# A two-layer transformer trunk on one core: the rotary embedding as three VectorE operations in place of twelve on GpSimd

## What is computed

```python
def apply_rope(t, cos, sin):
    half = ROT_DIM // 2                 # ROT_DIM = 32
    t1 = t[..., :half]
    t2 = t[..., half:ROT_DIM]
    return jnp.concatenate([t1 * cos - t2 * sin, t2 * cos + t1 * sin, t[..., ROT_DIM:]], axis=-1)

q = apply_rope(rms_norm(qkv[:, :, g, 0], q_gain[g]), cos, sin)      # layer 0, group g
k = apply_rope(rms_norm(qkv[:, :, g, 1], k_gain[g]), cos, sin)
k = rope_pairs(rms_norm((h @ w_k)..., k_gain), cos, sin)            # layer 1
q = rope_pairs(rms_norm((h @ w_q)..., q_gain), cos, sin)
```

## Time and profile before

| What | Value |
|---|---|
| median of three runs | 2704.87 us (2704.64, 2704.87, 2712.0) |
| span of the profiled execution | 2709.5 us |
| TensorE matmuls busy | 2437.8 us (90%), 10901 |
| TensorE weight loads busy | 1986.8 us (73%) |
| VectorE busy | 1856.3 us (69%), 2225 |
| ScalarE busy | 1152.7 us (43%), 1762 |
| GpSimd busy | 268.2 us (10%), 368 |
| mean DMA rate | 246 GB/s |
| w_lo, line 905 | 800 operations, 978.8 us |
| adaptive norm, line 924 | 194 operations, 457.2 us |

### The profile page before, as it was taken

One profiled execution on the slowest core, in us unless ns is written; L12 is line 12 of the kernel. 1 busy time (PEld: TensorE's weight loads), 2 busy tenths in 40 slices (PEclk: granted clock), 3 DMA queues, 4 the chain that ended last, 5 costly groups with the idle time before them and its releaser, 6 DMA issues.

```text
span 2709.5 us, 31158 instructions
## 1 busy us (share of the span) xinstructions
PE 2437.8 (90%) x10901; PEld 1986.8 (73%) x10901; DVE 1856.3 (69%) x2225; ACT 1152.7 (43%) x1762; POOL 268.2 (10%) x368
## 2 busy tenths in 40 slices
PE   0389989898899999999997768888899999999999
PEld 0378778776787888888886656766687888788887
DVE  7778676777778677777785657766887555455554
ACT  1345545454543443443444344444354344343442
POOL 1122121230100000000002341110000000000000
PEclk9699999999899999999998889999999999999999
DMA  9777575776788777787775556663977555555554
GB/s 362 283 262 287 221 294 210 304 268 215 282 301 312 268 287 265 276 309 246 280 290 199 205 191 249 257 246 132 351 278 265 187 190 182 172 186 186 188 186 155
DMA packets 150355, 665.66 MB, mean 246 GB/s; under 512 B 16752, under 2 KB 17104, under 8 KB 120784
## 3 DMA queue, kind: packets, MB, share of 16 engines
q1 hardware_dynamic: 150224, 663.95, 67.1%
HBM read 661.78 MB, written 2.10 MB: 245 GB/s over the span
## 4 chain that ended last, share of the span: by engine, by line
PE 63%; issue 16%; DVE 9%; POOL 8%; ACT 3%; DMA 2%; SPq 0%; DVEq 0%; POOLq 0%; ACTq 0%
PE main L384 20%; PE main L385 20%; PE main L386 20%; DVE acc L924 4%; POOL rot L1387 2%; POOL rot L1386 2%; DVE w_lo L905 2%; PE tr L397 2%; POOL rot L1388 1%; POOL rot L1389 1%; ACT w_hi L676 1%; DMA w_raw<-w 1%; POOL st_a L1393 1%; PE tr L439 1%; DMA ada_raw<-ada 1%
## 5 line engine op out<-in xcount | busy, mean ns | idle before, releaser
L905 DVE TENSOR_TENSOR w_lo<-w_raw,w_hi 128x1024 fp32r<-128x1024 f32 x800 | 978.8, 1228 | 625.7 <-ACT w_hi L676 624.6
L676 ACT ACTIVATE w_hi<-w_raw 128x1024 fp32r<-128x1024 f32 x800 | 847.0, 1061 | 1305.6 <-PE main L386 1171.5
L384 PE MATMUL main<-w_hi,hT_hi 128*128 128x512 f32 x2176 | 879.4, 404 | 9.0 <-DVE hT_lo L1081 4.0
L385 PE MATMUL main<-w_lo,hT_hi 128*128 128x512 f32 x2176 | 858.5, 395 | 3.9 <-issue 3.9
L386 PE MATMUL main<-w_hi,hT_lo 128*128 128x512 f32 x2176 | 857.3, 394 | 0.0
L384 PEld LDWEIGHTS main<-w_hi,hT_hi 128*128 128x128 f32 x2176 | 417.1, 192 | 98.4 <-DVE w_lo L905 6.0
L386 PEld LDWEIGHTS main<-w_hi,hT_lo 128*128 128x128 f32 x2176 | 415.2, 191 | 93.8 <-issue 4.1
L385 PEld LDWEIGHTS main<-w_lo,hT_hi 128*128 128x128 f32 x2176 | 416.6, 191 | 84.5 <-issue 1.2
L924 DVE SCALAR_TENSOR_TENSOR acc<-ada_raw,c_act,acc 128x2048 f32<-128x2048 f32 x194 | 457.2, 2357 | 7.1 <-DMA ada_raw<-ada 5.6
L384 PE MATMUL main<-w_hi,mid_hi 128*128 128x512 f32 x1024 | 405.8, 396 | 0.0
L386 PE MATMUL main<-w_hi,mid_lo 128*128 128x512 f32 x1024 | 403.6, 394 | 0.0
(11 more groups left out here) (161 smaller groups left out, 1340.7 us busy)
## 6 DMA issues: line engine op xcount, KB each, us to landing
w_raw<-w SPq DMA_DIRECT2D x800, 512.0 KB, 4.2
ada_raw<-ada SPq DMA_DIRECT2D x208, 1024.0 KB, 6.3
qT<-ada SPq DMA_DIRECT2D x16, 1024.0 KB, 6.9
gate<-bias_rows SPq DMA_DIRECT2D x4, 1024.0 KB, 7.2
xs<-x SPq DMA_DIRECT2D x1, 2048.0 KB, 9.9
out<-xs SPq DMA_DIRECT2D x4, 512.0 KB, 5.2
gains_sb<-gains SPq DMA_DIRECT2D x1, 640.0 KB, 4.5
st_a<-lamb SPq DMA_DIRECT2D x1, 256.0 KB, 5.5
```

Source lines behind the costliest of these rows:

```text
L384: pe.matmul(acc_ps[:, :], hi[:, kt, tc], w_hi[:, s, wc], start=(kt == 0), stop=False)
L385: pe.matmul(acc_ps[:, :], hi[:, kt, tc], w_lo[:, s, wc], start=False, stop=False)
L676: act.activation(w_hi[:, s, :], w_raw[:, s, :], ACT.Copy).then_inc(hi_done, 1)
L905: dve.tensor_tensor(w_lo[:, s, :], w_raw[:, s, :], w_hi[:, s, :].bitcast(F32), ALU.subtract).then_inc(lo_done, 1)
```

## The change

The tables become `cos8` and `sin8`, filled for all eight pairs of tile and head (128x256 each): the cosine twice in 32 columns, the sine once negated and once not. ScalarE fills them with six operations in place of two. The rotary embedding moves from GpSimd's queue into VectorE's `norm` step, right behind the normalization: a product of the first 32 elements of the eight heads with `cos8`, a product of the same elements with their halves swapped with `sin8`, and the sum of both in place. `read_out`, which frees the PSUM banks, is signalled by the first product, which waits for the norm's last operation; the sum waits for both products and signals `roped`. GpSimd keeps its other work (the staging of x and of the heads, line 1367). `rot` moves to another place in SBUF and is 128x512.

```diff
@@ tables
-        cos = sb("cos", [P, T * HALF])
-        sin = sb("sin", [P, T * HALF])
+        cos8 = sb("cos8", [P, T * MAPS, ROT])
+        sin8 = sb("sin8", [P, T * MAPS, 2, HALF])
-        rot = sb("rot", [P, T, 4, MAPS, HALF])
+        rot = sb("rot", [P, 2, T * MAPS, ROT])
@@ ScalarE, at the start
-            act.activation(sin[:, :], small[:, 0:T * HALF], ACT.Sin)
-            act.activation(cos[:, :], small[:, T * HALF:2 * T * HALF], ACT.Sin, bias=hpi_t[:, :],
-                           scale=-1.0).then_inc(trig_done, 1)
+            for t in range(T):
+                ang = small[:, t * HALF:(t + 1) * HALF].unsqueeze(1)
+                mag = small[:, (T + t) * HALF:(T + t + 1) * HALF].unsqueeze(1)
+                maps = slice(t * MAPS, (t + 1) * MAPS)
+                act.activation(sin8[:, maps, 0, :], ang.to_broadcast([P, MAPS, HALF]), ACT.Sin, scale=-1.0)
+                act.activation(sin8[:, maps, 1, :], ang.to_broadcast([P, MAPS, HALF]), ACT.Sin)
+                last = act.activation(cos8[:, maps, :].rearrange("p m (h e) -> p (m h) e", h=2),
+                                      mag.to_broadcast([P, 2 * MAPS, HALF]), ACT.Sin, bias=hpi_t[:, :], scale=-1.0)
+            last.then_inc(trig_done, 1)
@@ VectorE, norm
-                    last.then_inc(read_out[par], 1)
+                    chained(last)
+                    rotary = st_a[:, :].rearrange("p (m e) -> p m e", e=HD)[:, :, 0:ROT]
+                    swapped = rotary.rearrange("p m (h e) -> p m h e", h=2)[:, :, ::-1, :]
+                    dve.tensor_tensor(rot[:, 0], rotary, cos8[:, :, :], ALU.mult).then_inc(read_out[par], 1)
+                    chained(dve.tensor_tensor(rot[:, 1].rearrange("p m (h e) -> p m h e", h=2), swapped,
+                                              sin8[:, :, :, :], ALU.mult))
+                    dve.tensor_tensor(rotary, rot[:, 0], rot[:, 1], ALU.add).then_inc(roped, 1)
@@ GpSimd
-            def rope(par):
...
-                    pool.tensor_tensor(rot[:, t, 0], t1, c, ALU.mult)
-                    pool.tensor_tensor(rot[:, t, 1], t2, s, ALU.mult)
-                    pool.tensor_tensor(rot[:, t, 2], t2, c, ALU.mult)
-                    last = pool.tensor_tensor(rot[:, t, 3], t1, s, ALU.mult)
-                chained(last)
...
-                last.then_inc(roped, 1)
...
-            with repeat(pool, GROUPS, n, ro0=3, ro1=3, seq=4):
-                group()
```

More of the change, by code:

```diff
@@ L1245, in _ @@
             dve.wait_ge(consts, 3)
-            with repeat(dve, GROUPS - 1, n, w=6 * PIECES, ada=KT, landed=KT, col=4, seq=12, rms=4, qk=8, sc=8, pt=8, ov=4) as g:
+            with repeat(dve, GROUPS - 1, n, w=6 * PIECES, ada=KT, landed=KT, col=4, seq=20, rms=4, qk=8, sc=8, pt=8, ov=4) as g:
                 group(g, False)
@@ L1376, in head_rows @@
                          rden[:, (PK * j + k) * T + t:(PK * j + k) * T + t + 1]) for t in range(T) for k in range(PK)]
-            def rope(par):
[L1380 to L1385, removed]
-                    pool.tensor_tensor(rot[:, t, 0], t1, c, ALU.mult)
-                    pool.tensor_tensor(rot[:, t, 1], t2, s, ALU.mult)
-                    pool.tensor_tensor(rot[:, t, 2], t2, c, ALU.mult)
-                    last = pool.tensor_tensor(rot[:, t, 3], t1, s, ALU.mult)
-                chained(last)
[L1391 to L1394, removed]
-                last.then_inc(roped, 1)
-            def passed(par):
-                n[f"ro{par}"].up()
             chained(pool.memset(ident[:, :], 0.0))
@@ L1452, in _ @@
                 stage(range(2 * quad, 2 * quad + 2), head_rows)
-            n["ro0"].up(2)
-            n["ro1"].up(2)
-            pool.wait_ge(x_rstd, 2)
+            for update in (2, 3):
+                pool.wait_ge(x_rstd, update)
+                stage(range(PIECES), x_rows)
             stage(range(PIECES), x_rows)
[L1457 to L1470, removed]
             n["hT"].up(PIECES)
-            n["ro0"].up(2)
-            n["ro1"].up(2)
             pool.wait_ge(x_rstd, 4)
```

## The result

The changed kernel takes 2619.36 us (median; 2615.96 to 2620.64), the kernel before 2706.17 us on the same chip (2704.64 to 2712.0): a ratio of 0.9669, interval 0.9657 to 0.9681. That is 87 us between the medians and 90 us by the ratio. The forecast was 2610 us with a range of 2598 to 2630. Between the two profiled executions the span went from 2709.5 to 2618.9 us: -90.6 us, against 94.8 predicted.

What follows compares the result with a forecast made beforehand. TensorE was taken to be held by line 460 waiting for GpSimd's rotary embedding, 87.3 us in 20 waits. 103.4 - 4.7 - 0.3 - 2.6 - 1.0 = 94.8 us; 2704.9 - 94.8 = 2610 us, range 2598 to 2630.

Steps and rivals of the forecast that it cites:

- Long waits: Eleven waits of TensorE at line 460 for GpSimd's last rotary operation, 6.81 to 9.62 us; removal gives at most 103.4 us.
- six plain blocks: Six column blocks of 96 matmuls with one long wait each: 54.0 us to gain, 41.1 waiting and 12.9 slow clock.
- r: Time the three new rotary operations take in VectorE's queue at each embedding, put at 1.23 us.
- Rivals 3 and 4: Rotary operations slower on VectorE: r 4.3 us, 2650 us, chance 0.05; or r 7.5 us, 2717 us, chance 0.02.
- rival 5: The norm, not the embedding, is late, so the change doesn't reach the wait: no gain, 2706 us, chance 0.02.
- three shortest waits: Line 460 waits of 0.34 to 0.36 us, four score products before the transposes: 0.87 us lost each, 2.6 us.
- six short waits: Line 460 waits of 1.00 to 1.11 us: these go, but r delays the value product (line 488) 1.2 us; 0 each.
- The start: ScalarE fills the tables with six operations instead of two, before the squares of x: 1.0 us lost (0.5 to 2).
- VectorE's idle time less r: Limit on shrinking three norm-to-mask stretches in layer 1's last blocks: 8.7, 8.4 and 7.2 us, 4.7 us lost in all.
- rival 2: Another resource caps each of the eleven long waits at 7.2 us: gain 75.6 us, 2629 us, chance 0.07.
- last block's 3.35 us: Loss at layer 1's stretch of 30.42 us: it can shrink 7.2 us against a ceiling of 10.55.
- wait of 9.62 us: Longest line 460 wait, where the norm itself is late and room is only just r: 0.3 us lost.

Runs made afterwards that it cites:

- Experiment 4: Changed kernel with three adaptive-norm pieces (one load and one accumulate each) moved to earlier places: 2606.65 us, ratio 0.962 to the kernel before.
- Experiment 1: Changed kernel without its three rotary operations, two one-column memsets giving the signals: 2603.37 us, ratio 0.9605 to the kernel before.
- experiment 5: Changed kernel with the first score's mask ahead of the norm in VectorE's queue and two accumulates a piece later: 2609.09 us, ratio 0.9622 to the kernel before.
- experiment 2: Changed kernel with one more VectorE operation of 1.22 us between norm and rotary products: 2642.64 us, ratio 0.9751 to the kernel before.

## Why the prediction was right, and where it wasn't

- **Long waits, their slow clock, and the six plain blocks: right.** 54.0 us predicted, 54.0 measured. The price was the difference to a block of the same work without a wait, not the sum of the waits; that put in the 2.14 us of slow clock behind each.
- **r = 1.23 us: right** (1.25), from dense rows of the same engine and operation. Rivals 3 and 4 had r = 4.3 and 7.5; rival 5 needed the norm to be late. (The 11.7 us of the second embedding are 189.03 - 177.22 = 11.8; nothing rests on them.)
- **r shows where the queue has no room: right in kind.** 2.6 us were predicted at the three shortest waits and 2.4 measured (0.81, 0.81, 0.73). The second score product was to wait 1.7 us and waits 1.80. At the six short waits the value product was to wait about 1.2 us, with nothing lost in sum; it waits 0.30 to 0.93 us (3.9 us in all), three of the six blocks are 0.6 us shorter and three 0.1. The start was to cost 1.0 and costs 1.2.
- **The cap by "VectorE's idle time less r": the step that failed.** It said that a stretch from norm to masks can shrink until VectorE is full. It took idle time for free time. For the stretch of 32.30 us it gave 8.7 us and left 0.8 us of loss, for that of 34.08 us 8.4 and 0.55. They shrank by 6.2 and 7.1 us, and the blocks in which they end grew by 5.04 and 4.07 us. Their windows before, and after:

```profile
1639.00:1668.85 29.85, 28.46 (x121) 21.79 (x121) 17.27 (x36) 13.29 (x27) 0.00 (x0) 1.00 0.69 274
1773.50:1802.36 28.86, 26.90 (x130) 21.92 (x129) 18.67 (x38) 14.00 (x27) 0.00 (x0) 1.00 0.67 266
```

```profile
1569.90:1604.79 34.89, 30.15 (x122) 22.39 (x121) 19.69 (x36) 14.23 (x28) 0.00 (x0) 0.95 0.65 251
1690.60:1723.53 32.93, 28.56 (x130) 23.33 (x129) 19.86 (x39) 14.68 (x28) 0.00 (x0) 0.95 0.61 238
```

  The three stretches of the earlier trace rows in the changed kernel (windows of VectorE: length, busy, clock, DMA share, GB/s):

```profile
1553.37:1579.51 26.14, 23.10 (x22) 1.00 0.80 291
1672.84:1699.81 26.97, 25.16 (x30) 1.00 0.80 302
1734.20:1757.11 22.91, 22.70 (x39) 1.00 0.84 310
```

  In the third VectorE is full, and there the rule held. In the first two it stands still for 3.0 and 1.8 us, nearly all of it for loads of ada_raw (2.94 and 1.61 us). Waits of after from 1553 to 1580, that of ScalarE, then those of the load queue:

```profile
ACT w_hi L676 <- DMA w_raw<-w: 11.2, 3, 5.6
```

```profile
SPq L275 <- DVE w_lo L911: 14.6, 4, 5.1
SPq L285 <- DVE acc L930: 9.9, 3, 3.7
```

  and VectorE's timeline:

```profile
1570.92 2.35 DVE L930 SCALAR_TENSOR_TENSOR acc<-ada_raw,c_act,acc 128x2048 f32<-128x2048 f32 x1 [2.10 <-DMA ada_raw<-ada]
1573.27 1.23 DVE L911 TENSOR_TENSOR w_lo<-w_raw,w_hi 128x1024 fp32r<-128x1024 f32 x1
1575.34 2.35 DVE L930 SCALAR_TENSOR_TENSOR acc<-ada_raw,c_act,acc 128x2048 f32<-128x2048 f32 x1 [0.84 <-DMA ada_raw<-ada]
...
1578.88 0.29 DVE L1021 CUSTOM_DVE_ANT_0 sm<-sc,masks 128x128 f32<-128x128 f32 x1
```

  and SyncE's issues of the two loads that these accumulates wait for:

```profile
1563.71 0.33 SPq L285 DMA_DIRECT2D ada_raw<-ada  x1
...
1567.71 0.33 SPq L285 DMA_DIRECT2D ada_raw<-ada  x1
```

  ada_raw has two slots. Each load was issued right at the end of the accumulate two before it (1563.69 and 1567.68), and is used 7.2 and 7.6 us after its issue, at a mean DMA share of 0.80. SyncE's queue holds both kinds of load in one order; in this stretch it stands for 14.6 us until a w_raw slot is free and for 9.9 us until an ada_raw slot is, and whatever is behind waits too, so that w_hi is late as well. The mask at 1578.88, for which TensorE waits, stands behind all that. Before, the long wait of TensorE lay in this stretch, and in it the loads landed: the one accumulate that waited did so for 0.36 us. The second part of the miss is the clock: of the 9.1 us, 5.8 us are the growth of the two waits of TensorE (3.40 from nothing, 3.03 from 0.61), and 3.3 us are TensorE's longer busy time, 1.7 us in each block, for the same work: slow clock, which the sum had put at nothing here. Windows of after behind the first:

```profile
1580.50:1583.90 3.40, 3.40 (x5) 1.36 (x5) 2.08 (x7) 0.06 (x1) 0.00 (x0) 0.50 1.00 404
```

  Experiment 4 takes all of the growth away by the places of the sums. Experiment 1 takes 1.4 and 1.0 us of the waits by r. How much is the loads and how much VectorE's own work ahead of the mask (23.10 of 26.14 us) is told by the traces alone, 2.94 us of idle time against a wait of 3.40, and by no experiment of its own. Nor does a run tell whether more slots or faster transfers would have helped. The mechanism is rival 2's, another resource as cap, but at two blocks and not at eleven: the plain blocks carry a DMA share of 0.90 and 0.88 without a wait.
- **The last block's 3.35 us: nearly right.** The same rule gave 7.2 us, the stretch shrank by 7.5 and its block by 7.52. The block behind it got 1.27 us shorter besides; there a wait of 2.6 us, which was followed by slow clock before, is followed by none now.
- **The wait of 9.62 us: a missed step.** 0.3 us of loss was predicted, from a ceiling of 11.8, and the block shortened by 7.41 (waiting now 2.77, with slow clock behind it). TensorE's transposes of the second half need the second bank of tr, which VectorE frees at line 1110. In its queue r, a w_lo and an accumulate stand ahead of that; VectorE's timeline, and TensorE's wait:

```profile
1535.85 0.42 DVE L1004 TENSOR_TENSOR st_a<-rot 128x256 f32<-128x256 f32 x1
1536.19 1.22 DVE L911 TENSOR_TENSOR w_lo<-w_raw,w_hi 128x1024 fp32r<-128x1024 f32 x1
1537.33 2.35 DVE L930 SCALAR_TENSOR_TENSOR acc<-ada_raw,c_act,acc 128x2048 f32<-128x2048 f32 x1
...
1539.62 0.06 DVE L1110 MEMSET marks<- 128x1 f32 x1
```

```profile
1539.75 1.11 PE L460 MATMUL tr<-ident,st_a 128*128 128x128 f32 x4 [2.77 <-DVE marks L1110]
```

  The prediction asked who waits for the norm's end, and not what else stands behind r in the queue. Experiment 1 left 1.7 of the 2.8 us, experiment 4 0.5: it is mostly the accumulate.
- **Sum.** The terms missed by more than the sum. Too much gain was forecast in the two blocks with masks (7.7 us) and at the wait of 9.62 us (11.8 - 0.3 - 7.4 = 4.1 us); too little in the last block and the one behind it (1.6), the short waits (2.2) and the rest (3.7). What is left is 4 us; that misses of 12 us one way and 7.5 us the other cancel so far was luck. The other 5 us between 2610 and 2619 are in how the median stands to the profiled span: 4.6 us below it before (with a fourth run 3.3), level with it now.

## What to carry to other kernels

Price a wait by comparing the block that holds it with one of the same work that doesn't; then ask of every engine and load queue what it did during the wait. Idle time of an engine is room only if what it would do next can arrive sooner too: look at which loads land during the wait that you remove. And before moving work to a faster engine, try to move its reader later: here that alone gave 70 of 90 us (by ratio), and with VectorE a place in the queue (experiments 4 and 5) was worth about as much as the operations themselves (experiment 1).

## What the runs showed of the hardware beside that

- Some short waits cost clock too, and the length of the wait doesn't tell which. Behind the new wait of 2.77 us, as behind one of 2.06 us in experiment 2, the granted clock was 0.50 (1.2 GHz) for the 3.4 us shown; behind that of 1.80 us it stayed at 1.00. But in experiment 2 it also stayed at 1.00 behind a wait of 2.99 us, and in the changed kernel it was 0.50 from 1614.6 to 1618.0, behind waits of 1.45 and 0.59 us. The same wait of line 471 was followed by slow clock with 3.40 us in the changed kernel and by none with 3.08 us in experiment 5. Windows of after, and of experiment 2 behind the wait of 2.99 us:

```profile
1539.50:1542.90 3.40, 3.15 (x10) 2.67 (x11) 3.40 (x5) 0.00 (x0) 0.00 (x0) 0.50 0.33 102
224.40:227.80 3.40, 3.31 (x16) 2.81 (x17) 3.40 (x10) 0.00 (x0) 0.00 (x0) 1.00 0.45 149
```

```profile
225.60:229.00 3.40, 3.35 (x16) 2.83 (x17) 3.40 (x8) 0.00 (x0) 0.00 (x0) 1.00 0.61 218
```

- The prediction weighed a rule of the Trainium skill (SBUF — State Buffer, SBUF: two separate sides) by which VectorE would gain once GpSimd is silent. The 800 w_lo have 974.7 us against 978.8 before, so the sign is right, and the size is 4 us of VectorE's busy time in the whole run. It is GpSimd that was stretched, to 2.37 us for an operation that also took 0.31.
